# A fifth block of half products in the front, and unsplit native fp32 values in the paged attention

## The reference, cut to what matters

```python
h = rms_norm(x, attn_norm)
z = jnp.einsum('btd,de->bte', h, w_in)              # one combined input projection
q_a, ckv, krope, u, qm, gate = jnp.split(z, SPLIT_POINTS, axis=-1)
...
def mla_attend(q_lat, q_rope, ckv, krope, mask):    # sample: 8 sequences, 16 pages of 128 rows each
    s = einsum('bthr,bsr->bhts', q_lat, ckv) + einsum('bthe,bse->bhts', q_rope, krope)
    p = softmax(where(mask, s, -inf))
    return einsum('bhts,bsr->bthr', p, ckv)
```

## Time and profile before

| | us |
| --- | --- |
| median of 3 runs | 854.45 (854.42 to 854.62) |
| the profiled execution | 854.57 |
| its span in the trace | 852.9 |
| PE busy | 844.0 |
| DVE busy | 657.0 |
| ACT busy | 499.0 |
| POOL busy | 148.4 |

### The profile page before, as it was taken

The page is one execution under the profiler, slowest core; times in us unless marked ns, Lnnn a source line. Parts: engine busy times, 40 slices in busy tenths (PEclk is TensorE's granted clock), DMA queues, the critical chain, the costliest instruction groups (busy, mean ns, idle before and its releaser), DMA issues.

```text
span 852.9 us, 15840 instructions
## 1 busy us (share of the span) xinstructions
PE 844.0 (99%) x5453; PEld 768.0 (90%) x5453; DVE 657.0 (77%) x1044; ACT 499.0 (59%) x829; POOL 148.4 (17%) x213
## 2 busy tenths in 40 slices
PE   9999999999999999999999999999999999999996
PEld 9999999988998999999999999888887788888885
DVE  6998885788538769888888866967679889464777
ACT  7577443634433557776766755577787546363446
POOL 0000001463100122333333340000001012111123
PEclk9999999999999999999999999999999999999999
DMA  9526317544666487788888755424047685979586
GB/s 345 199 86 237 108 52 275 173 131 148 213 259 238 158 274 244 255 278 270 265 260 259 227 179 198 170 82 152 20 149 276 152 239 102 268 199 280 110 152 222
DMA packets 64879, 168.57 MB, mean 198 GB/s; under 512 B 9672, under 2 KB 27657, under 8 KB 62808
## 3 DMA queue, kind: packets, MB, share of 16 engines
q1 hardware_dynamic: 52672, 126.46, 43.0%
q0 software_dynamic: 10752, 33.56, 17.2%
q10 hardware_dynamic: 1376, 7.54, 2.5%
HBM read 156.14 MB, written 11.50 MB: 197 GB/s over the span
## 4 chain that ended last, share of the span: by engine, by line
PE 99%; ACT 0%; issue 0%; DVE 0%; POOL 0%; ACTq 0%; DVEq 0%; POOLq 0%
PE front_acc L94 9%; PE front_acc L96 9%; PE front_acc L95 9%; PE z L94 8%; PE z L96 7%; PE z L95 7%; PE pa_s L94 4%; PE pa_s L96 4%; PE pa_s L95 4%; PE pa_qk L96 3%; PE pa_qk L95 3%; PE pa_qk L94 3%; PE ps_o L1773 2%; PE ps_o L1774 2%; PE ps_s L1727 2%; PE pa_t L96 2%
## 5 line engine op out<-in xcount | busy, mean ns | idle before, releaser
L94 PE MATMUL z<-x_hi,w_hi 128*128 128x288 f32 x480 | 142.7, 297 | 0.0
L96 PE MATMUL z<-x_hi,w_lo 128*128 128x288 f32 x480 | 141.3, 294 | 0.0
L95 PE MATMUL z<-x_lo,w_hi 128*128 128x288 f32 x480 | 141.3, 294 | 0.0
L214 ACT ACTIVATE w_hi<-w_raw 128x1024 fp32r<-128x1024 f32 (+2 forms) x52 | 54.5, 1048 | 88.1 <-PE z L96 39.2
L1322 POOL DMA_DIRECT2D v_raw<-in_cache x128 | 69.0, 539 | 163.3 <-issue 161.7
L2352 ACT ACTIVATE o_hi<-o_raw 128x1024 fp32r<-128x1024 f32 x50 | 52.9, 1060 | 69.8 <-PE pa_s L3326 33.1
L94 PEld LDWEIGHTS z<-x_hi,w_hi 128*128 128x128 f32 x480 | 90.1, 188 | 2.7 <-issue 1.1
L221 DVE TENSOR_TENSOR w_lo<-w_raw,w_hi 128x1024 fp32r<-128x1024 f32 (+2 forms) x52 | 67.3, 1294 | 31.7 <-ACT w_hi L214 31.4
L95 PEld LDWEIGHTS z<-x_lo,w_hi 128*128 128x128 f32 x480 | 90.1, 188 | 1.7 <-issue 0.2
L96 PEld LDWEIGHTS z<-x_hi,w_lo 128*128 128x128 f32 x480 | 90.0, 188 | 0.0
L2606 DVE TENSOR_TENSOR o_lo<-o_raw,o_hi 128x1024 fp32r<-128x1024 f32 x50 | 60.9, 1221 | 33.9 <-ACT o_hi L2352 33.8
(11 more groups left out here) (628 smaller groups left out, 2530.5 us busy)
## 6 DMA issues: line engine op xcount, KB each, us to landing
k_raw<-in_cache SPq DMA_DIRECT2D x128, 192.0 KB, 3.4
w_raw<-in_w_feat SPq DMA_DIRECT2D x40, 512.0 KB, 4.7
v_raw<-in_cache POOLq DMA_DIRECT2D x128, 128.0 KB, 3.5
o_raw<-in_w_out POOLq DMA_DIRECT2D x30, 512.0 KB, 8.4
o_raw<-in_w_out SPq DMA_DIRECT2D x20, 512.0 KB, 8.7
w_raw<-in_w_mem_kv SPq DMA_DIRECT2D x16, 512.0 KB, 3.4
mix<-gate_spill SPq DMA_DIRECT2D x4, 1152.0 KB, 10.7
x_row<-in_x ACTq DMA_DIRECT2D x4, 1024.0 KB, 4.7
```

The lines of the kernel that those rows point to most:

```text
L94: pe.matmul(out, a[0], b[0], start=start, stop=False, skip_group_check=onto)
L95: pe.matmul(out, a[0], b[1], start=False, stop=False, skip_group_check=onto)
L96: return pe.matmul(out, a[1], b[0], start=False, stop=stop, skip_group_check=onto)
L214: act.activation(hi_slot(s, u)[:, lo:w], s.wraw[:, raw_slot(u), lo:w], ACT.Copy).then_inc(s.w_hi, 1)
```

## The change

**A fifth block.** `PAIRS` goes from 4 to 5: the gate tiles 0 and 1 are done in the front by seven half products (28 products become 35). They leave the middle, so that `FEATS` goes from 20 to 18 and the middle's parts from 60 to 52: the 12 among the query work stay, `STEPS` stays 38, and only steps 14 and 37 are long. The fifth block's partial sums lie in a raw slot of the ring (so unit 11's load waits until they are read), DVE scales them, ACT takes the sigmoid, DVE multiplies, and SP stores the two tiles. Loads of the units after the products are timed by the same distances from the end of the products, and the last two front units swap their high slots, so that unit 30 waits for unit 28 to end where it waited for unit 27.

**Values.** `v_hi`, `v_lo` and the low part of the turned probabilities are gone. `probs_t` is plain fp32 with 64 columns a page. A page's values are one native fp32 matmul of 256 columns with 64 stationary columns; even pages write partitions 0 to 63 of `ps_o`, odd pages 64 to 127. The new rows are two native matmuls with 64 rows and 128 columns each, one for each half. ACT's and DVE's work at the end, which adds the two halves, is as before.

```diff
-PGATE, GATE, QM = range(0, 4), range(5, 17), (4, 17, 18, 19)
-FEATS, FRONT = 20, 5
+PGATE, GATE, QM = range(0, 4), range(5, 15), (4, 15, 16, 17)
+FEATS, FRONT = 18, 5
...
-PAIRS, TERMS = 4, 7
+PAIRS, TERMS = 5, 7
...
-RING_FREE = (23, 25, 27, 28)
+RING_FREE = (29, 32, 34, 35)
...
-    before = u - (HI if u < FIRST + SPL else SPL)
+    before = u - {FIRST - 2: HI - 1, FIRST - 1: HI + 1}.get(u, HI if u < FIRST + SPL else SPL)
...
+            sp.wait_ge(st_add, OWN_READY + 1)
+            load_units(sp, a, s, 11, 12)
...
+                    if n_ == PAIRS - 1:
+                        dve.wait_ge(st_add, OWN_READY - 1)
+                        dve.tensor_tensor(own_gates[:, 0, :], s.wraw[:, RING_SLOT[3], 0:T], rbf, ALU.mult).then_inc(st_add, 1)
...
+                if j in (5, 6):
+                    act.wait_ge(st_add, OWN_READY + j - 5)
+                    act.activation(bend(6 - j), own_gates[:, j - 5, :], ACT.Sigmoid).then_inc(st_cp, 1)
...
+                if j in (6, 7):
+                    dve.wait_ge(st_cp, 3 * PAIRS + j - 5)
+                    v = own_gates[:, j - 6, :]
+                    dve.tensor_tensor(v, v, bend(7 - j), ALU.mult).then_inc(st_add, 1)
...
-LONG = (*range(2, 29, 3), STEPS - 1)
+LONG = (14, STEPS - 1)
...
-        pt = at("probs_t", [P, NPAGE + 1, 2 * NS], F32R)
+        pt = at("probs_t", [P, NPAGE + 1, NS])
...
-            def values_hi(m):
-                act.wait_ge(v_in[m % VRING], 64 * (m // VRING + 1))
...
-            def values_lo(m):
-                dve.wait_ge(v_hi, m + 1)
...
-                    pe.wait_ge(v_lo, m + 1)
+                    pe.wait_ge(v_in[m % VRING], 64 * (m // VRING + 1))
                     for j in range(4):
-                        g = 4 * (m % 4) + j
-                        pe.matmul(p_o[:, 0:KVR], pt[:, g, :], vh[:, m % HRING, j, :], start=g == 0, stop=False)
-                        last = pe.matmul(p_o[:, 0:KVR], pt[:, g, :], vlo[:, m % VRING, j, :], start=False, stop=False)
+                        g, o = 4 * (m % 4) + j, NS * (j % 2)
+                        last = pe.matmul(p_o[o:o + NS, 0:KVR], pt[:, g, :], vraw[:, m % VRING, j, :], start=g < 2, stop=False)
                     if m % 4 == 3:
-                        pe.wait_ge(zeros, 3)
-                        pe.matmul(p_o[:, 0:KVR], pt[:, 16, :], vs_hi[:], start=False, stop=False)
-                        last = pe.matmul(p_o[:, 0:KVR], pt[:, 16, :], vs_lo[:], start=False, stop=True)
+                        for c in range(2):
+                            last = pe.matmul(p_o[NS * c:NS * c + NS, P * c:P * c + P], pt[0:NS, NPAGE, :],
+                                             s.kvn[0:NS, 4, P * c:P * c + P], start=False, stop=True)
```

More of the change, by code:

```diff
@@ L79 @@
 TERM_ROLE = "abYXcZd"
-GATE_TILE = list(range(8, 12)) + list(range(0, 8)) + list(range(12, 16))
+PAIR_TILE = (0, 1)
+GATE_TILE = list(range(8, 12)) + list(range(2, 8)) + list(range(12, 16))
 GT = 3
@@ L195, in hi_slot @@
     if u >= FIRST:
-        return high(s, u % SPL)
-    return high(s, u % HI if u < TAKEN else (u + 1) % HI)
+        return high(s, (u + 1) % SPL)
+    if u < TAKEN:
+        return high(s, u % HI)
+    return high(s, ((u if u < FIRST - 2 else 2 * FIRST - 3 - u) + 2) % HI)
 def hi_free(eng, s, u):
@@ L378, in target @@
                 return s.zq[:, 2 * n + i, TH * half:TH * half + TH]
+            if n == PAIRS - 1:
+                at_ = TH * (2 * i + half - i)
+                return s.wraw[:, RING_SLOT[3], at_:at_ + TH]
+            if n == 3 and i == 1:
+                return u_late[:, TH * half:TH * half + TH]
             return U(2 * (n - 2) + i)[:, UPAD + TH * half:UPAD + TH * half + TH]
@@ L472, in _ @@
                         sp.dma_start(dst, src).then_inc(out, 16)
+                if u == 16:
+                    for i in range(2):
+                        sp.wait_ge(st_add, OWN_READY + 2 + i)
+                        sp.dma_start(s.spill[PAIR_TILE[i]], own_gates[:, i, :]).then_inc(out, 16)
                 if u == 21:
@@ L690, in _ @@
                     act.wait_ge(m_chain, 6)
-                    act.wait_ge(out, 16 * (6 + DB))
+                    act.wait_ge(out, 16 * (8 + DB))
                     for i in range(2):
@@ L890, in _ @@
                     finish_u(1)
+                if step == 29:
+                    finish_u(2)
                 if step == 23:
@@ L1370, in _ @@
             act.activation(sq[:, :, old], s.zq[:, :, old], ACT.Square).then_inc(squared, 1)
-            act.activation(vs_hi[0:NS, :], s.kvn[0:NS, 4, 0:KVR], ACT.Copy).then_inc(vs_done, 1)
             act.wait_ge(chain, 1)
@@ L1437, in _ @@
                         act.wait_ge(ot_sb, 2 * (b - 1))
-                    act.activation(pt[:, 16, 0:NS], p_m[:, own(b - 1)], ACT.Copy).then_inc(pt_hi, 1)
+                    act.activation(pt[:, 16, :], p_m[:, own(b - 1)], ACT.Copy).then_inc(pt_sb, 1)
                 if n == STEPS - 1:
@@ L1577, in _ @@
             dve.wait_ge(msk_in, 32)
[L1578 removed]
+            dve.wait_ge(zeros, 4)
             for n_ in range(STEPS):
```

121 lines of the change are left out of this document (53 added, 68 removed).

## The result

The changed kernel takes **863.83 us** (median of 4 runs, 863.59 to 864.82) where the kernel before, timed beside it, takes 854.54 (854.42 to 854.64). The ratio is 1.0111, 95% interval 1.0093 to 1.0128: 9.3 us slower, where 5.5 were forecast. The profiled execution has a span of 862.2 us.

What follows compares the result with a forecast made beforehand. TensorE's queue was taken as the bound, PE's waits being only 1.6 us. Fifth block -3.2, values +8.2 and new rows +0.5 gave +5.5 us: 860.0 us against 854.45, 0.6% slower, range 852 to 868.

Steps and rivals of the forecast that it cites:

- the main term: Values in the middle: each quad 0.257 us longer in the new form, +8.2 us over 32 quads.
- the likeliest case: Whole kernel: the forecast as summed holds, 857 to 863 us, chance 0.62.
- The price of the shape: TensorE, around each quad: entering and leaving the 64-column shape loses a constant 0.35 us (bounds 0.33 and 0.49).
- The cheap switch: Quads: entering and leaving the shape hides behind weight loads and queue, a quad 0.856 us, total 848 us; chance 0.16.
- staggered tiles: Quads: second tile starts one pass late, 0.107 us more on each of 32, +3.4, total 863.5 us; chance 0.10.
- no concurrency: Quads: the two halves never run side by side, 0.86 us more each, +27 us, total 888; chance 0.02.
- Quads and new rows: Values on TensorE: a quad 0.949 to 1.206 us, new rows 0.237 to 0.294 us; +8.2 and +0.5 us.
- The block's matmuls: TensorE: middle loses 8 parts, front gains 7 products of the same 24 matmuls, 3.20 us each; net -3.2 us.
- the nearest miss: Front, unit 30's high slot: about 0.2 us to spare; if missed, a few tenths of a us once.
- "I cost all of this at nothing": Fifth block's other work in the front (splits, sums, scaling, gates, stores, unit 11's load), and later the middle's loads: 0 us.
- My fourth rival: Middle: shorter steps make PE wait for scores, keys or values, 0.2 us in 32 steps, +6.4, 866.5 us or more; 0.10.
- The cover: Middle: dropping value splits frees ACT 33.6 and DVE 38.8 us, no direct gain, but room for shorter steps; DVE below 16 us.

Runs made afterwards that it cites:

- the last kernel: Next unit's copy and subtraction put behind the key splits, against four quads in one stay with rope tables loaded first and late tanh: 852.63 us, ratio 0.9976.
- the tables (-1.2): Rope tables and latent gain issued before the wait and unit 11's load, against the kernel with four quads in one stay: 857.75 us, ratio 1.0036.
- the version with split values: Kernel before plus the fifth block, values still split, with long steps 2 and 37, rope tables loaded first and late tanh: 860.53 us, ratio 1.0073.

## Why the prediction was right, and where it was short

The direction and the main term were right for the reason given. The size was short by 3.8 us: 863.8 lies inside the range of 852 to 868, but just outside the 857 to 863 of the likeliest case.

**The price of the shape: right.** It was taken from a block of 16 long instructions, one of 16 in four tiles and one of 64 short ones, and put on blocks of 8. A quad measured 1.205 us. The runs with stays added and taken away gave 0.36 us each. With all four quads in one stay, a stretch of four steps without a wait took 22.71 us (in the last kernel) where the changed kernel has 23.73, 0.34 for each of the three stays that are gone. So the price does not depend on the length, from 4 to 32 instructions. What would have made the prediction wrong, a price that depends on what stands ahead and behind, did not show either. From the first matmul with `k_lo` of a step to that of the next, the kernel with the values alone against the kernel before, 20 steps with a quad and no new rows grew by 0.24 to 0.28 us, 0.27 in the mean; those with transposes ahead of the quad are no exception (0.25 to 0.28).

**The cheap switch, staggered tiles, no concurrency: excluded.** A quad would have been 0.86, 1.31 and 2.06 us. The total alone would have misled: the staggered tiles had 863.5 us, next to the 863.8 that were measured. That is an accident: the 3.4 us that they put into the quads are not there, and some 3.2 us of waits elsewhere are.

**Quads and new rows: a little small.** A quad grew by 0.27 us and not 0.257, and a step with the new rows by 0.34, so that the new rows have about 0.08 where 0.057 was forecast. The eight sequences came to 9.2 us and not 8.7.

**The block's matmuls: right.** Parts stayed at 3.17 to 3.20 us, the front grew by 22.07, a steady stretch is 23.73. Unit 30, the nearest miss by the prediction, did not make PE wait.

**"I cost all of this at nothing": the step that failed**, for the front's loads and for the splits in the middle, with 1.0 and 2.2 us. In the front I followed the load that now waits for DVE to what it loads (unit 11, three units ahead of its use, which was right) and not to what is issued behind it on the same queue, the tables. These hold POOL's rope and then a window operation, which runs beside a `mem_lo` of DVE and delays it by 1.1 us. The 58.85 of 84 us that DVE is busy in the memory units promised room; but that is a mean, and behind this place DVE has none for 43 us. In the middle I compared the load of DVE with the length of a steady step, 16.29 of 23.73 us, and concluded that PE does not wait; in steady steps it does not. In steps 2 to 4, which have no quad and no longer a long step among them, the order of the work on ACT and DVE makes a chain that is longer than the step: 5.8 us in step 4, which took 4.8 without a wait. My fourth rival, that shorter steps make PE wait, was right there and wrong in the other steps, and its price of 0.2 us in each of 32 steps was wrong. The numbers are shown by the kernel with the long step at 2 (-2.0), and by the tables (-1.2).

**The cover: right.** With the splits left in, the block costs 9.7 us in place of saving 3.2. Adding up single costs, +9.3 for the values and +9.7 for the block, would give 19; together they are 9.3, since the first frees the engine that the second overloads.

**Left open:** 0.25 us in the last stage, how PE pairs pages that are not neighbours, and which part of the waits in the version with split values is load and which is order. Nothing was run to price the block in the front apart from its loads.

## What to carry to other kernels

Here the tile shape had a price for each stay and not for each instruction: count the stays, and put together what can be put together before judging the form by its streaming rate. When a step gets shorter, compare it with the longest chain on the other engines from the event that starts it to the event that PE needs, not with their busy share, and put last what nobody is waiting for. When a load gains a wait, follow everything that its queue issues behind it.

## What the runs showed of the hardware

- A stay in 64-column tiles amid full-shape matmuls cost 0.34 to 0.38 us at 4, 8, 16 and 32 instructions of 256 columns, which take 0.108 us each beyond it. Native fp32 amid fp32r in the full shape cost nothing on the way in and out (L1678, 0.86 us for two instructions of 0.428).
- The order of the four pages in a quad made no difference (864.55 us against 863.83; a quad 1.09 us against 1.08 in the timeline), though in one order neighbours in the queue are for the same half of the array.
- DVE is held up by POOL. While POOL runs its windows, one subtraction of 128x1024 takes 2.40 us and not 1.23, and a `mem_lo` 1.59 and not 0.48; in DVE's timeline after, the rows inside and just outside of POOL's two window rows above are these:

```profile
193.84 0.48 DVE L803 SCALAR_TENSOR_TENSOR mem_lo<-mem_raw,g_mem,mem_hi 128x256 fp32r<-128x256 f32 x1
194.23 2.40 DVE L225 TENSOR_TENSOR w_lo<-w_raw,w_hi_more 128x1024 fp32r<-128x1024 f32 x1
196.55 1.59 DVE L803 SCALAR_TENSOR_TENSOR mem_lo<-mem_raw,g_mem,mem_hi 128x256 fp32r<-128x256 f32 x1
...
200.64 1.23 DVE L225 TENSOR_TENSOR w_lo<-w_raw,w_hi 128x1024 fp32r<-128x1024 f32 x1
```

The Trainium skill, GPSIMD Engine Reference, Specifications, has GpSimd's SBUF interfaces shared with VectorE, with contention for DVE instructions in a 2-port performance mode or with two SBUF inputs. By that, the trace agrees: the subtraction has two tensors from SBUF, and so has `mem_lo`. That entry gives no size; here both instructions are 1.1 to 1.2 us longer, whatever their own length, so it is a delay and not a factor.
